# Reordered heads of stages in a two-layer trunk: which slab is gated first, where the third slab's weight split stands, and who adds the last chunk's squares

## The reference, cut to what matters

```python
for i in range(DEPTH):
    mod = (e @ ada_w[i] + ada_b[i][None, :]).reshape(B, N_SUBLAYERS, N_MOD, D_MODEL)
    shift, scale, gate = mod[:, :, 0], mod[:, :, 1], 1 + mod[:, :, 2]
    h = modulate(x, norm_g[i, 0], shift[:, 0], scale[:, 0])
    x = x + 0.5 * gate[:, 0][:, None, :] * swiglu(h, ffn_w1[i, 0], ffn_w3[i, 0], ffn_w2[i, 0])
    h = modulate(x, norm_g[i, 1], shift[:, 1], scale[:, 1])
    ...
    x = x + gate[:, 1][:, None, :] * y
    h = modulate(x, norm_g[i, 2], shift[:, 2], scale[:, 2])
    x = x + 0.5 * gate[:, 2][:, None, :] * swiglu(h, ffn_w1[i, 1], ffn_w3[i, 1], ffn_w2[i, 1])

def rms_norm(x, g):
    y = xf * lax.rsqrt(jnp.mean(xf * xf, axis=-1, keepdims=True) + EPS)
def modulate(x, g, shift, scale):
    return rms_norm(x, g) * (1 + scale[:, None, :]) + shift[:, None, :]
def swiglu(h, w1, w3, w2):
    return (jax.nn.silu(h @ w1) * (h @ w3)) @ w2
```

## Time and profile before

| | |
|---|---|
| median of 3 runs | 2016.26 us (2015.67 to 2016.7) |
| the profiled execution | 2016.22 us, of it span 2014.4 us |
| TensorE busy | 1965.3 us (98% of the span), 9750 matmuls |
| VectorE busy | 1101.2 us (55%) |
| ScalarE busy | 661.7 us (33%) |
| GpSimd busy | 144.2 us (7%) |
| DMA | 275.88 MB, mean 137 GB/s |
| mean granted TensorE clock | 0.99 |

### The profile page before, as it was taken

The page is one execution under the profiler, slowest core; times in us unless marked ns, Lnnn a source line. Parts: engine busy times, 40 slices in busy tenths (PEclk is TensorE's granted clock), DMA queues, the critical chain, the costliest instruction groups (busy, mean ns, idle before and its releaser), DMA issues.

```text
span 2014.4 us, 24679 instructions
## 1 busy us (share of the span) xinstructions
PE 1965.3 (98%) x9750; PEld 1593.4 (79%) x9750; DVE 1101.2 (55%) x1344; ACT 661.7 (33%) x742; POOL 144.2 (7%) x96
## 2 busy tenths in 40 slices
PE   6899999999989999999999999999999999999999
PEld 4688888886577888888788888887897887888887
DVE  3766554589877565633666533345559764333322
ACT  3422232242254222222422322224238744223211
POOL 0100000121411000001100000101012120000000
PEclk8999999999989999999999999999999999999999
DMA  9345444526413454433254422232235422222222
GB/s 397 150 170 205 169 186 158 175 91 186 127 53 136 179 196 181 181 121 100 105 201 174 188 98 81 92 124 105 84 84 126 120 89 84 104 88 100 86 89 96
DMA packets 50777, 275.88 MB, mean 137 GB/s; under 512 B 7456, under 2 KB 8096, under 8 KB 25760
## 3 DMA queue, kind: packets, MB, share of 16 engines
q1 hardware_dynamic: 47648, 270.87, 38.0%
q10 hardware_dynamic: 3072, 4.23, 0.8%
HBM read 251.94 MB, written 2.10 MB: 126 GB/s over the span
## 4 chain that ended last, share of the span: by engine, by line
PE 88%; DVE 5%; ACT 3%; DMA 1%; issue 1%; SPq 0%; POOL 0%; DVEq 0%; ACTq 0%
PE ps L1394 27%; PE ps L1395 27%; PE ps L1396 27%; PE ps L1612 2%; DMA stage<-ada_d 1%; DVE w L856 1%; PE ps L1733 1%; PE ps L1747 1%; DVE h_lo L999 1%; ACT h_hi L650 1%; PE ps L1720 1%; PE ps L1501 1%; PE ps L1479 1%; DVE sq_tmp L996 0%; DVE w L1041 0%
## 5 line engine op out<-in xcount | busy, mean ns | idle before, releaser
L1394 PE MATMUL ps<-h_hi,w 128*128 128x512 f32 x1648 | 649.6, 394 | 17.6 <-DVE w L1041 12.9
L1395 PE MATMUL ps<-h_lo,w 128*128 128x512 f32 x1648 | 643.2, 390 | 0.0
L1396 PE MATMUL ps<-h_hi,w 128*128 128x512 f32 x1648 | 642.9, 390 | 0.0
L1394 PEld LDWEIGHTS ps<-h_hi,w 128*128 128x128 f32 x1648 | 310.5, 188 | 95.5 <-DVE w L1041 14.6
L1396 PEld LDWEIGHTS ps<-h_hi,w 128*128 128x128 f32 x1648 | 310.5, 188 | 65.6
L1395 PEld LDWEIGHTS ps<-h_lo,w 128*128 128x128 f32 x1648 | 310.8, 189 | 62.8
L856 DVE TENSOR_TENSOR w<-raw,w 128x1408 fp32r<-128x1408 f32 (+1 forms) x101 | 189.3, 1874 | 210.2 <-ACT w L606 210.2
L606 ACT ACTIVATE w<-raw 128x1408 fp32r<-128x1408 f32 (+1 forms) x101 | 158.9, 1573 | 426.5 <-PE ps L1396 420.6
L1394 PE MATMUL ps<-g_hi,w 128*128 128x512 f32 x704 | 274.2, 390 | 0.0
L1396 PE MATMUL ps<-g_hi,w 128*128 128x512 f32 x704 | 273.9, 389 | 0.0
L1395 PE MATMUL ps<-g_lo,w 128*128 128x512 f32 x704 | 273.9, 389 | 0.0
(11 more groups left out here) (204 smaller groups left out, 1645.5 us busy)
## 6 DMA issues: line engine op xcount, KB each, us to landing
raw<-up_d SPq DMA_DIRECT2D x88, 1024.0 KB, 6.3
ada_raw<-ada_d SPq DMA_DIRECT2D x64, 1024.0 KB, 4.8
raw<-down_d SPq DMA_DIRECT2D x64, 704.0 KB, 4.1
raw<-mix_d SPq DMA_DIRECT2D x28, 1024.0 KB, 4.7
stage<-ada_d SPq DMA_DIRECT2D x12, 1024.0 KB, 20.9
stk<-parted SPq DMA_DIRECT2D x32, 256.0 KB, 4.3
stk<-parted SPq DMA_DIRECT2D x32, 128.0 KB, 2.3
u_blk<-u SPq DMA_DIRECT2D x48, 64.5 KB, 2.0
```

Of the source, the lines that this page charges most:

```text
L1394: pe.matmul(dst, a_hi_, b_hi_, start=start, stop=False, skip_group_check=True)
L1395: pe.matmul(dst, a_hi_, b_lo_, start=False, stop=False, skip_group_check=True)
L1396: return pe.matmul(dst, a_lo_, b_hi_, start=False, stop=stop, skip_group_check=True)
```

## The change

The change has four parts.

First, in the first feed-forward (m=0) slab 1 is gated before slab 0. VectorE no longer makes the shift sums at the end of the head: it multiplies slab 1's product, does the first half of a modulation block, splits slab 3, and only then makes the shift sums, keeps the bias, does the block's second half and gates slab 0. TensorE's `bias_sums` move from inside slab 2 to between slabs 2 and 3, and the reduction that stood at the third chunk of slab 3 stands at the fifth.

Second, in the other feed-forwards (m=3, 4, 6) ScalarE casts slab 2 between the fourth and the fifth normalised chunk, not after slab 0's gating, and VectorE subtracts its low part before the gating of slab 0.

Third, in the QKV stage (m=5) VectorE subtracts slab 2's low part before it takes slab 0's product out of the accumulator. TensorE's third slab now waits for the two factor products too, since it overwrites what they read.

Fourth, for every m but 0 and 2 GpSimd also adds the last chunk's squares (a seventh step), `sums` has one set of four narrow products instead of two, and it stands one chunk later in slab 0 (`k == 3`).

```diff
         def ss_steps(m):
-            return 6 * m
+            return 6 * m + (m > 1) + max(0, m - 3)
...
             def squares(m, c):
-                if c == 0 or c == KD - 1:
+                if c == 0:
                     return
...
-                    if m == 0 and c == 3:
-                        hi(N_UP[0] + 2)
+                    if m in FFN_ENTRY and c == 3:
+                        hi(FIRST[m] + 2)
...
             def ffn(j, m, nxt, last=False):
                 nb = Q_BODIES[j]
-                for s in range(2):
-                    up_step(j, 0, s, split=(j > 0 or s > 0), first=FFN_ENTRY[j] if s == 0 else None)
+                if j == 0:
+                    up_step(0, 0, 1, turn=0)
+                    up_step(0, 0, 0, split=False, first=0, turn=1)
+                else:
+                    for s in range(2):
+                        up_step(j, 0, s, split=s > 0, first=FFN_ENTRY[j] if s == 0 else None)
...
                     lo(N_UP[0] + 2)
-                    dve.wait_ge(h_odd_done, 3)
-                    shift_sums(0)
-                    keep_bias(0)
...
                     for b in range(2 if first else 0):
                         first_factor(first, up_tmp[b], pair[0][b]).then_inc(u0_done, 1)
+                    if first:
+                        lo(n + 2)
                     dve.wait_ge(silu_done, f + 1)
...
+                if between:
+                    between()
                 dve.wait_ge(ghi_done, f + 1)
...
+                if j == 0:
+                    def first_half(s):
+                        dve.wait_ge(ada_s, 16 * (2 * Q_FFN[0] - 11 + s))
+                        ada_half(Q_FFN[0], s, ada_raw, ada_acc[:, :])
+
+                    up_step(0, 0, 1, False, turn=0, between=lambda: first_half(0))
+                    dve.wait_ge(h_odd_done, 4)
+                    dve.wait_ge(g_done, 1)
+                    shift_sums(0)
+                    keep_bias(0)
+                    first_half(1)
+                    up_step(0, 0, 0, False, split=False, first=0, turn=1)
...
                 if s == 0:
+                    lo(n + 2)
                     for b in range(2):
                         first_factor(5, qk[:, b, :], pair[0][b]).then_inc(u0_done, 1)
...
-                if s < 11:
+                if 0 < s < 11:
                     lo(n + 2)
...
-                    if k == (2 if m else 5):
+                    if k == (3 if m else 5):
                         sums(m)
...
+                if m:
+                    pe.wait_ge(ss_step, ss_steps(m) + 7)
+                    add(ss, True, True, stat_done)
+                    return
...
                 if m == 0:
-                    for s in range(2):
-                        up_step(j, 1, s, None, True, lambda: bias_sums(0))
+                    up_step(j, 1, 0, None, True)
+                    bias_sums(0)
+                    up_step(j, 1, 1, None, True, 4)
...
                 pe.wait_ge(lo_done, n + 1)
+                if s == 2:
+                    pe.wait_ge(u0_done, 2 * ENTRY[5] + 2)
```

More of the change, by code:

```diff
@@ L650, in h_his, with up_step @@
                         act.activation(h_hi[:, c, :], t_buf(c), ACT.Identity, bias=shift).then_inc(hhi_done, 1)
-                    if m == 0 and c == 3:
-                        hi(N_UP[0] + 2)
-            def up_step(j, i, s, split=True, first=None):
+                    if m in FFN_ENTRY and c == 3:
+                        hi(FIRST[m] + 2)
+            def up_step(j, i, s, split=True, first=None, turn=None):
                 n = N_UP[j] + 2 * i + s
@@ L665, in up_step @@
                     act.activation(tmp, pair[s][0], ACT.Silu).then_inc(silu_done, 1)
-                act.wait_ge(g_full, KF * j + 2 * i + s + 1)
+                act.wait_ge(g_full, KF * j + 2 * i + (s if turn is None else turn) + 1)
                 act.activation(g_hi[:, 2 * i + s, :], tmp, ACT.Copy).then_inc(ghi_done, 1)
@@ L1019, in x_add, with up_step @@
                                          op0=ALU.mult, op1=ALU.add).then_inc(x_done, 1)
-            def up_step(j, i, s, ada, split=True, take=True, first=None):
+            def up_step(j, i, s, ada, split=True, take=True, first=None, turn=None, between=None):
                 n = N_UP[j] + 2 * i + s
-                f = KF * j + 2 * i + s
+                f = KF * j + 2 * i + (s if turn is None else turn)
                 tmp = act_tmp[:, s, :]
@@ L1042, in up_step @@
                         .then_inc(lo_done, 1)
-                elif first != 0:
+                elif first is None:
                     lo(N_DOWN[j] + s, DOWN)
@@ L1053, in ffn @@
                 nb = Q_BODIES[j]
-                for s in range(2):
-                    up_step(j, 0, s, bool(nb), split=(j > 0 or s > 0), take=False, first=FFN_ENTRY[j] if s == 0 else None)
+                if j == 0:
[9 more added lines that the diff above has]
+                    up_step(0, 0, 0, False, split=False, first=0, turn=1)
+                else:
+                    for s in range(2):
+                        up_step(j, 0, s, bool(nb), split=s > 0, take=False, first=FFN_ENTRY[j] if s == 0 else None)
                 if nb:
@@ L1475, in sums, with add @@
             def sums(m):
-                def add(src, first, sem_):
+                def add(src, first, stop, sem_):
                     for c in range(4):
                         last = pe.matmul(row[:, c:c + 1], src[:, c * P:(c + 1) * P], ones[:, 0:1],
-                                         start=(first and c == 0), stop=not first, skip_group_check=True)
+                                         start=(first and c == 0), stop=stop, skip_group_check=True)
                     if sem_ is not None:
                         last.then_inc(sem_, 1)
+                if m:
+                    pe.wait_ge(ss_step, ss_steps(m) + 7)
+                    add(ss, True, True, stat_done)
+                    return
                 pe.wait_ge(ss_step, ss_steps(m) + 6)
-                add(ss, True, None)
+                add(ss, True, False, None)
                 pe.wait_ge(sq_done, KD * m + KD)
-                add(sq_tmp[:, 1, :], False, stat_done)
+                add(sq_tmp[:, 1, :], False, True, stat_done)
             def spread(m):
```

5 lines of the change are left out of this document (2 added, 3 removed).

## The result

The changed kernel takes 1998.25 us (median of 4 runs, 1997.39 to 1998.68), the kernel before 2016.22 us beside it. The ratio is 0.991, 95% interval 0.9897 to 0.9922: 18.0 us (0.9%) faster. The profiled execution took 1997.39 us with a span of 1995.6 us, 18.8 us less than before.

The account below looks back on a forecast made before the run. TensorE, busy 98% of the span, was taken as the bound, so only less work or shorter waits help. Terms 7.5 + 3.6 + 3.4 + 2.0 - 0.5 - 1.5 = 14.5 us off 2016.22 gave 2001.7 us, range 1999 to 2006.5.

Parts of the forecast that it names:

- The first feed-forward: At m=0, slab 3's wait of 5.9 us goes whole and 1.6 us of low clock with it: 7.5 us gained.
- Slab 2 of m=3, 4, 6: In these three heads slab 2 starts 2.0 us earlier each, with 1.3 us of TensorE's wait remaining.
- The clock's return: At slab 2 of m=3 and m=4, the clock no longer falls behind the wait: 1.6 and 1.4 us gained.
- m=1 and the length of the wait at m=5: Before slab 2, waits grow to 1.9 us at m=1 (term -0.46 us) and 2.4 us at m=5 (start unchanged).
- The fall at m=5: At slab 2 of m=5, the clock falls behind the wait grown to 2.4 us: 1.5 us lost, taken whole.
- (a): Rival: no fall of the clock at slab 2 of m=5, so 2000.2 us; chance 0.22.
- (b): Rival: clock also falls behind remaining waits at m=1, 3, 4, 6, costing 3 to 6 us: 2004.7 to 2007.7; chance 0.15.
- (c): Rival: hoisted cast starves slab 1 at m=3, 4, 6, so 9.0 us don't come: 2010.7 us; chance 0.07.
- (d): Rival: GpSimd's seventh step holds TensorE in slab 0 of five heads, making it slower: 2017.7 us; chance 0.03.
- (e): Rival: at m=0 the wait only moves, to slab 4 or the bias sums, losing half of 7.5 us: 2005.5; chance 0.06.
- the rest: Outcomes the forecast couldn't name, including a gain of more than (a) gives; chance 0.05.

Follow-up runs that it names:

- e1_gate: Kernel before with only the first feed-forward's part (slab 1 gated first at m=0): 2008.32 us, ratio 0.9959.
- e4_nostats: Changed kernel with the statistics part undone (two sets of narrow products, at the third chunk, six steps on GpSimd): 1997.98 us, ratio 0.9909.
- e7_fill: Changed kernel plus 16 matmuls with unused results in the two waits at the convolution module's end: 1999.40 us, against 1999.13 for the changed kernel beside it.
- e2_cast: Kernel before with only the hoisted casts and low parts of slab 2 at m=3, 4, 6: 2005.85 us, ratio 0.9951.
- e9_before: Kernel before, unedited, measured and profiled once more as a second sample: 2018.38 us.

## Why the prediction was right, and where not

**The first feed-forward: right.** 7.5 us were forecast. 436.16 against 443.33 is 7.17 us, which is 7.6 less the 0.46 us of m=1. Slab 3 starts at 75.78 (75.8 in the text), slab 4's low part ends at 86.6 (86.6). The numbers that the text gives for a slab's length add up to 11.1 us, not to its 10.9. It did no harm: TensorE came to slab 4 at 87.33 (87.1 in the text), 0.7 us behind the low part. `e1_gate` gives the same 7.7 us by itself.

**Slab 2 of m=3, 4, 6: right.** 2.0 us each; the profile has 2.05, 2.05 and 1.97, with 1.10 us of wait left instead of 1.3. From slab 0 to slab 2 of m=3 it takes 623.95 - 598.94 = 25.0 us, as written. The clock's return, 1.53 and 1.37 us at m=3 and m=4, is the 1.6 and 1.4 of the sum. Over three profiles the clock fell behind 6 of 9 such waits, the two in three that the sum held, though spread in another way.

**m=1 and the length of the wait at m=5: right, with one size off.** 1.77 us for 1.9, 2.25 for 2.4. The set of narrow products that falls away was put at 0.9 us of TensorE, but from slab 0 to slab 1 of m=3 it takes 12.87 us instead of 13.62, so it gave 0.75. With that, 0.57 + 0.46 + 0.75 is 1.78, 1.50 + 0.75 is 2.25, and the 1.3 us forecast at m=3, 4 and 6 become 1.1, as measured. It moved no term of the sum, since what TensorE saves there turns into wait. Slab 2 of m=5 neither gained nor lost a start.

**What failed.** The time lies below the range by two steps: a term that the sum put at nothing without a reason, the attention's transfers (1.6 us), and a term entered whole that comes only in some executions, the fall at m=5 (1.0 us).

**The fall at m=5: failed in size.** The wait grows to 2.4 us, "the length behind which the clock fell twice of three", and the sum takes the whole 1.5 us off. The fall didn't come in the first profile. Over the three it came once, at a price of 1.4 us (the two profiles are 1.69 us apart at m=5 and 3.11 at 1508.09). What had a chance of two in three by the rows then known, and came once in three since, had been entered as a full term. The mean price is about 0.5 us, so 1.0 us of the 3.3 to 3.5 us that were missing is this.

**What the sum left out: the larger step that failed.** It adds up the edited heads only, and so takes every other place as unchanged, without a reason for it. The attention's transfers were not: 1.9 us of wait on average before, 0.3 after. That is the larger part of the gap, 1.6 us. It goes with the statistics part, by the count of profiles above and by `e4_nostats`, where undoing that part brings the wait back. Why a late issue moves with it stays open. The end of the convolution module gave 1.6 us in the first pair of profiles, but 24.25 against 23.96 us on average over three. The other kernels' profiles lie between 23.3 and 24.5 us there (`e1_gate` 23.27, `e4_nostats` 24.48), so the 0.3 us is no gain that is shown. It goes with the clock: the five profiles with a low stretch of 13.7 us there (all kernels but `e7_fill`) took 24.5 us, the seven with 10.2 us took 22.9 to 23.8. Together: 14.5 + 1.0 + 1.6 = 17.1 us, and with these 0.3 us 17.4, beside 17.8 between the mean spans (2014.8 and 1997.0) and 18.0 between the medians. The few tenths left are within what the first 64 us of these profiles differ by from run to run (63.75 to 64.81 at slab 2 of m=0).

**The rivals.** (a), no fall at m=5, described the first profile, but its 2000.2 us had neither of the two other entries. The time lies in what the forecast called the rest, more than (a) gives, at a chance of 0.05. (b) didn't happen: no wait from 1.1 to 1.8 us had a fall behind it in any profile. (c) is refuted by `e2_cast` and by the 2.05 us. (d), GpSimd late, didn't happen: the seventh add took 1.30 us and had 1.1 us to spare. What got longer was VectorE's `entry_low` beside it, 1.28 us at 601.20 against 0.75 before, and TensorE doesn't wait for that one. (e) is refuted by 75.78 and 86.6. The forecast saw that the statistics part lengthens the chain by 0.46 us a head, but not what it costs alone: 6.7 us, since it pushes waits of 2.4 to 3.6 us, and in that profile each then has its fall. In the changed kernel the hoist had shortened the waits first; what the part still costs the heads there, 1.8 us, the attention's transfers give back.

## What to carry to other kernels

Work taken from the busiest engine is worth nothing in a stretch at whose end that engine waits for another; ask first what the chain it waits for begins with, and start that sooner. Here the statistics part cost 6.7 us alone and about nothing in the changed kernel, and the changed kernel with its sum one chunk earlier was 5.8 us faster still. An effect that comes in some executions only is entered in a sum with its chance, not as a whole term; and a small gap against the sum is looked for in places that no edit touched, by taking the same kernel's profile more than once.

## What the hardware showed unexpectedly

The fall of TensorE's clock behind a wait of 2.2 to 2.4 us isn't a property of the kernel: it came behind 8 of 12 waits of 2.4 us (three profiles of the kernel before and `e1_gate`) and behind one of three waits of 2.2 us in the changed kernel, whose lengths agree to 0.02 us. In `e9_before` it came after the restart, at m=3 and at m=6, where the first matmul still took 0.50 us, so that row doesn't tell whether the clock fell; the windows behind it do (granted clock 0.50 from 1676 to 1678 us, the wait ended at 1674.16). At the end of the convolution module it began under work, while TensorE ran products of one moving column without a break. A VectorE subtraction of two 128x2048 inputs took 3.32 and 3.34 us beside a GpSimd subtraction of 128x512, 2.29 alone. One issue of a transfer took 1.5 to 1.9 us instead of 0.60 at the same place in six profiles of four kernels, and an edit to other engines' programs moved the late issues to other places.
